# Expert gathers as f32 products straight from the residual, with one more home for weight halves

## The reference

```python
def expert_choice_swiglu(h, w_router, w_gate, w_up, w_down):
    cap = EC_CAPACITY_FACTOR * seq // N_EXPERTS            # 64 tokens per expert, 16 experts
    aff = jax.nn.softmax(jnp.einsum('bsd,de->bse', h, w_router), axis=-1)
    g, idx = lax.top_k(jnp.swapaxes(aff, 1, 2), cap)
    xin = jax.vmap(lambda hb, ib: hb[ib])(h, idx)          # gather
    a = jnp.einsum('becd,edf->becf', xin, w_gate)
    u = jnp.einsum('becd,edf->becf', xin, w_up)
    y = jnp.einsum('becf,efd->becd', jax.nn.silu(a) * u, w_down) * g[..., None]
    return ...zeros.at[idx].add(y)                         # scatter
# x = x + attention part;  x = x + expert_choice_swiglu(rms_norm(x, norm2_g), ...);  rms_norm(x, normf_g)
```

## Time and profile before

| | us |
|---|---|
| time, median of 3 runs | 874.66 (874.02 to 877.3) |
| the profiled execution's own time | 872.47 |
| its span, first to last instruction | 870.7 |
| TensorE busy | 846.2 (97%) |
| VectorE busy | 373.5 (43%) |
| ScalarE busy | 264.8 (30%) |
| GpSimd busy | 29.0 (3%) |
| granted TensorE clock, mean | 0.996 of full speed |
| read from HBM | 235.92 MB |

### The profile page before, as it was taken

How to read it: one execution, slowest core, us unless ns; L and a number is a source line. 1 busy time by engine, 2 the same in 40 slices (tenths; PEclk the granted TensorE clock), 3 DMA queues, 4 the chain that set the end, 5 groups by cost and what they waited for, 6 DMA issues and landing times.

```text
span 870.7 us, 10464 instructions
## 1 busy us (share of the span) xinstructions
PE 846.2 (97%) x4239; PEld 516.6 (59%) x4239; DVE 373.5 (43%) x650; ACT 264.8 (30%) x460; POOL 29.0 (3%) x50
## 2 busy tenths in 40 slices
PE   9999999999999999999999999999999998988996
PEld 8898776687878888888634344344433433334432
DVE  5377977576605335416412146322232231311351
ACT  6234776685634234216011011010100101001231
POOL 1050000000000000001100000000000000000010
PEclk9999999999999999999999999999999999999999
DMA  9730212023133425863999999999999999999996
GB/s 287 172 97 0 74 48 98 1 68 90 43 119 109 118 67 141 293 260 129 424 408 422 428 427 430 427 426 426 429 428 428 429 425 429 427 428 429 425 416 265
DMA packets 81427, 239.20 MB, mean 275 GB/s; under 512 B 8038, under 2 KB 63462, under 8 KB 66788
## 3 DMA queue, kind: packets, MB, share of 16 engines
q1 hardware_dynamic: 75952, 235.94, 68.7%
q10 hardware_dynamic: 5284, 2.09, 1.0%
q0 software_dynamic: 144, 0.51, 0.1%
HBM read 235.92 MB, written 2.62 MB: 274 GB/s over the span
## 4 chain that ended last, share of the span: by engine, by line
PE 79%; DMA 12%; DVE 5%; ACT 2%; issue 1%; POOLq 0%; POOL 0%; SPq 0%; ACTq 0%; DVEq 0%
PE psum L1622 18%; PE psum L1654 11%; PE psum L1150 10%; PE psum L1152 10%; PE psum L1151 10%; DMA wslot<-in_w_down 7%; DMA wslot<-in_w_up 4%; PE psum L1579 3%; PE psum L1673 2%; PE psum L1338 2%; PE psum L1350 2%; PE psum L1782 2%; PE psum L1308 1%; PE psum L1324 1%; DVE w_lo L1855 1%
## 5 line engine op out<-in xcount | busy, mean ns | idle before, releaser
L1622 PE MATMUL psum<-wslot,xinT 128*64 128x512 f32 x1000 | 222.1, 595 | 4.3 <-DMA wslot<-in_w_up 2.5
L1622 PEld LDWEIGHTS psum<-wslot,xinT 128*64 128x64 f32 x1000 | 69.5, 137 | 141.9 <-issue 132.7
L1654 PE MATMUL psum<-wslot,actT 128*64 128x512 f32 x424 | 96.0, 596 | 5.0 <-DMA wslot<-in_w_down 5.0
L1150 PE MATMUL psum<-hT_hi,w_hi 128*128 128x512 f32 x208 | 82.8, 398 | 0.0
L1152 PE MATMUL psum<-hT_hi,w_lo 128*128 128x512 f32 x208 | 81.3, 391 | 0.0
L1151 PE MATMUL psum<-hT_lo,w_hi 128*128 128x512 f32 x208 | 81.3, 391 | 0.0
L1855 DVE TENSOR_TENSOR w_lo<-w_raw,w_hi 128x1024 fp32r<-128x1024 f32 (+1 forms) x46 | 52.9, 1174 | 51.0 <-ACT w_hi L787 50.9
L1654 PEld LDWEIGHTS psum<-wslot,actT 128*64 128x64 f32 x424 | 29.2, 137 | 61.4 <-issue 57.3
L1083 ACT ACTIVATE actT<-psum 128x512 f32<-128x512 f32 x16 | 9.6, 599 | 172.7 <-PE psum L1634 172.7
L2261 DVE TENSOR_TENSOR x<-x,psum 128x512 f32<-128x512 f32 x48 | 29.8, 683 | 57.3 <-PE psum L1673 57.3
L2251 DVE TENSOR_TENSOR y_lo<-psum,y_hi 64x512 fp32r<-64x512 f32 x28 | 19.3, 689 | 81.1 <-ACT y_hi L1093 80.7
(11 more groups left out here) (287 smaller groups left out, 1335.3 us busy)
## 6 DMA issues: line engine op xcount, KB each, us to landing
wslot<-in_w_up SPq DMA_DIRECT2D x27, 2048.0 KB, 23.4
wslot<-in_w_gate SPq DMA_DIRECT2D x25, 2048.0 KB, 24.9
wslot<-in_w_down SPq DMA_DIRECT2D x24, 2048.0 KB, 22.0
w_raw<-in_w_in SPq DMA_DIRECT2D x34, 512.0 KB, 4.7
wslot<-in_w_gate SPq DMA_DIRECT2D x12, 1024.0 KB, 9.2
wslot<-in_w_up SPq DMA_DIRECT2D x9, 1024.0 KB, 10.6
wslot<-in_w_down SPq DMA_DIRECT2D x9, 1024.0 KB, 19.7
w_raw<-in_w_out SPq DMA_DIRECT2D x8, 512.0 KB, 4.9
```

What stands on the lines that cost most here:

```text
L1150: pe.matmul(out_, s_hi, m_hi, start=(k == 0), stop=False)
L1622: mm = pe.matmul(bank[2 * e + n][CAP * f:CAP * f + CAP, :], xinT[:, HALF * h + k, CAP * e:CAP * e + CAP], wslot[place_of(m)][:, k % PART, ...
L1654: mm = pe.matmul(bank[4 + e][CAP * f:CAP * f + CAP, :], actT[:, e, k, CAP * h:CAP * h + CAP], wslot[place_of(m)][:, k % PART, SEQ * f:SEQ ...
```

## The change

It removes the split of the residual. `pick`, `row_ids` and the new `aff_cols` become plain f32, and the gathers multiply pick by x2 itself in f32: 4 products of 512 columns where 8 in fp32r stood. The sums go into a tile of their own, `sums` at W0. The first gather of pair 0 is turned round: chunks of x2 are the stationary operand and pick the moving one, so the result comes transposed, without ACT's copy and TensorE's transposes; it goes chunk by chunk (four, two of them ahead of the gates, two between gate products). The later copies of rows are read by chunks with a step of 4.

The space of `xn_lo` becomes a ninth wide home (W0 + 16), SLOTS = 18, and the two single homes in x2's space move to W0 and W0 + 8. SyncE loads parts 20, 21 and 18 after the first four residual groups, part 19 after the second logits, all ahead of the wait for all groups; half 16 comes one place later.

```diff
-SLOTS = 16
-FIRST_PARTED, LAST_PARTED = (*range(8, 15), 16), range(92, 96)
+SLOTS = 18
+FIRST_PARTED, LAST_PARTED = range(9, 17), range(92, 96)
-EXTRA = {16: 16, 7: 17, 18: 18, 19: 19, 32: 18, 33: 19}
+EXTRA = {16: 18, 7: 19, 18: 20, 19: 21, 32: 20, 33: 21}
-                 enumerate((W0 + 32, 0, 16, W0 + 48, 32, 64, W0 + 64, W0 + 80))]
+                 enumerate((W0 + 32, 0, 16, W0 + 48, 32, 64, W0 + 64, W0 + 80, W0 + 16))]
-    wslot += [sb(f"wslot_once{i}", [PART, D], kib) for i, kib in enumerate((48, 56, 80, 88))]
-
-    xn_hi = sb("xn_hi", [NT, D], W0, F32R)
-    xn_lo = sb("xn_lo", [NT, D], W0 + 16, F32R)
+    wslot += [sb(f"wslot_once{i}", [PART, D], kib) for i, kib in enumerate((48, 56, W0, W0 + 8))]
+
+    sums = sb("sums", [NT, D], W0)
-    pick = sb("pick", [NT, 2, CAP], 100, F32R)
+    pick = sb("pick", [NT, 2, CAP], 100)
...
+        FIRST_BANKS = (6, 7, 4, 5)
...
-            sp.wait_ge(sumsq2, 2)
-            sp.wait_ge(x2_turned, 2)
-            sp.wait_ge(xn_lo_done, 4)
+            sp.wait_ge(proj_done, g_at[("res", 0, NT - 1)] + 1)
+            load_part(20)
+            load_part(21)
             load_part(18)
+            sp.wait_ge(logits_done, 2)
+            load_part(19)
             sp.wait_ge(proj_done, len(groups))
             for m in (7, 11, 12, 13, 14, 15, 16, 17):
                 load_part(m)
-
-            sp.wait_ge(sumsq2, NT + 1)
-            sp.wait_ge(x2_turned, NT + 1)
-            sp.wait_ge(xn_lo_done, 5)
-            sp.wait_ge(xn_lo_pool, len(LOW_BY_POOL))
-            load_part(19)
-            for half in (*range(10, 16), 17, 18, 16, *range(19, len(HALVES) * PAIRS)):
+            for half in (*range(11, 16), 17, 18, 19, 16, *range(20, len(HALVES) * PAIRS)):
...
-                    mm = pe.matmul(into[:, 0:6], pick[:, c, :, :], aff_parts[:, c, p, :, :],
+                    mm = pe.matmul(into[:, 0:3], pick[:, c, :, :], aff_cols[:, c, p, :],
...
+            def gather_first(k, tiles=range(NT)):
+
+                for c in tiles:
+                    pe.wait_ge(pick_done, c + 1)
+                    chunk = x2[:, c, 0:SEQ].rearrange("p (i k) -> p k i", k=HALF)[:, k, :]
+                    mm = pe.matmul(bank[FIRST_BANKS[k]][:, 0:P], chunk, pick[:, c, :, :],
+                                   start=(c == 0), stop=(c == NT - 1))
+                mm.then_inc(xin_turned, 1)
...
                 for c in range(NT):
-                    for part in (xn_hi, xn_lo):
-                        mm = pe.matmul(bank[6 + f][:, :], pick[:, c, :, :], part[:, c, cols],
-                                       start=(c == 0 and part is xn_hi), stop=(c == NT - 1 and part is xn_lo))
+                    mm = pe.matmul(bank[6 + f][:, :], pick[:, c, :, :], x2[:, c, cols],
+                                   start=(c == 0), stop=(c == NT - 1))
...
-                        steps.sort(key=lambda step: step[1] // PART)
+                        steps.sort(key=lambda step: step[1])
...
-            for c in range(NT):
-                pe.wait_ge(pick_done, c + 1)
-                gather_first(c, 0)
-            for c in range(NT - 1):
-                gather_first(c, 1)
-            turn_first_xin(0)
-            gather_first(NT - 1, 1)
+            gather_first(0)
+            gather_first(1)
...
-                    if step == 1:
-                        turn_first_xin(1)
+                    if step in (1, 3):
+                        gather_first(2 + step // 2)
...
-                pe.wait_ge(sum_lo_done, c + 1)
-                for part in (sum_hi, sum_lo):
-                    pe.matmul(row_sum(f), pick[:, c, :, :], part[:, c, SEQ * f:SEQ * f + SEQ],
-                              start=(c == 0 and part is sum_hi), stop=False, skip_group_check=True)
+                pe.matmul(row_sum(f), pick[:, c, :, :], sums[:, c, SEQ * f:SEQ * f + SEQ],
+                          start=(c == 0), stop=False, skip_group_check=True)
...
-                        dve.tensor_reduce(slot_vals[CAP * f:CAP * f + CAP, p % 2, e, :],
-                                          src[CAP * e:CAP * e + CAP, 0:6].rearrange("p (v s) -> p v s", s=2),
-                                          AX, ALU.add).then_inc(slot_aff_done, 1)
+                        dve.tensor_copy(slot_vals[CAP * f:CAP * f + CAP, p % 2, e, :], src[CAP * e:CAP * e + CAP, 0:3])\
+                            .then_inc(slot_aff_done, 1)
...
+                    before = sums if p else x2
+                    dve.tensor_tensor(sums[:, c, cols], before[:, c, cols], bank[added_bank(c, f)][:, :], ALU.add)\
+                        .then_inc(added, 1)
```

## The result

The changed kernel takes 901.29 us (median of 6, 898.6 to 903.09), beside 875.14 us for the kernel before (6 runs): a ratio of 1.0297, with a 95% interval of 1.0278 to 1.0317. It is slower by 26 us. The profiled execution took 898.88 us with a span of 897.0, 26.3 us over the 870.7 of before; the forecast was a span of 895.3, +24.6.

What follows compares the result with a forecast made beforehand. TensorE was taken to bound the kernel until stocked weights ran out in the sixth pair, then transfers. TensorE's +35.5 us less 10.9 us of waits gave +24.6, span 895.3; time 898.5 us, range 889 to 908.

Steps and rivals of the forecast that it cites:

- The race: Expert pairs: TensorE's pair grows from 52.61 to 56.6 us, still under the transfers' 58.8, so the 10.9 us of waits vanish.
- The f32 gather: Double gather of each expert pair on TensorE: 7.24 us in place of 3.76, +3.48 us; seven of them +24.4.
- The small ones: TensorE's smaller additions: pairing of rows +1.0 us, slot values +0.5 each, eight times, +4.0, last gather of rows +3.3.
- Routing: Routing stretch set by TensorE: dropped copies and subtractions gain 0, except the last aff value, -0.3 us.
- the first gather: First pair's gather on TensorE: gates start earlier, -0.5 us; two more chunks between gate products, +1.9 us.
- The sum: Whole span: TensorE's additions +35.5 us less 10.9 us of vanished waits, net +24.6 us, a span of 895.3.
- The step from 899.3 down to 898.5: Final time: lowered from 899.3 us against the median, as a kernel no longer waiting for transfers may vary less.
- The supply: Weight loads: four parts (9.8 us) move into the empty stretch 384 to 404 us; a 3 to 4 us hole after 427.1.
- transfers are some 2.5 us earlier: Net effect on weight transfers: some 2.5 us earlier, with 22 parts rather than 20 in hand when the gates start.
- Rival 1: Transfers set the end and longer gathers hide in TensorE's waits: not slower, 872 us; chance 0.05.
- rival 2: TensorE's waits for weights stay on top, through a late transfer or a larger hole at 427: 910 us; chance 0.08.
- rival 3: Wide f32 products on TensorE cost about 0.33 us a record, 15 us less: 884 us; chance 0.05.

Runs made afterwards that it cites:

- halved loads: Every load after a home's first tenant brings only half its bytes: changed kernel 900.10 us (ratio 1.0301), kernel before 862.67 us (0.9866).

## Why the prediction was right, point by point

**The race.** It rested on two rhythms, 52.6 us a pair on TensorE and 58.8 on the transfers, and on the reading that the 10.9 us of spacing is all that can be hidden. The halved loads gave 10.9 us by the medians and 10.7 by the chain. The pair was forecast at 56.6 us and is 56.4.

**The f32 gather.** Forecast +3.48 us a double gather, measured 6.97 - 3.76 = +3.21. The record is 6.97/16 = 0.436 with its share of the start, near my lower bound of 0.43. The start of 0.1 us was about right; the record of 0.444, half-width products of L1622 taken two at a time, was too long: inside the row six records span 2.74 us and one takes 0.592, which makes 0.429 from start to start. The Trainium skill (FP8 and Floating Point Precision, "TensorE Precision Notes") says that true FP32 takes four passes through the array; the trace comes near it, with 2 x 0.436 us for a product of 512 columns against 0.235 for an fp32r one, 3.7 times.

**The small ones.** Against the earlier trace rows, the slot values and the end:

```profile
828.05 1.09 PE psum L1669 x8
829.14 0.79 PE psum L1672 x8
...
865.55 1.91 PE psum L1678 x4
867.46 0.47 PE psum L1588 x4
867.93 1.72 PE psum L1678 x4
...
880.65 7.02 PE psum L1727 x32
```

Pairing 1.88 (forecast 1.94), slot values 0.79 (0.85), last gather of rows 1.91 + 1.72 + 1.91 + 1.91 = 7.45 in all, +3.1 (+3.3). Not forecast: the strided transposes of the pair, 1.16 in place of 1.02 us.

**Routing.** The aff value that had taken 0.98 us beside POOL takes 0.23 now that POOL's subtraction is gone, and the transpose that needs it follows TensorE's filler products without a wait, as read from the earlier trace rows:

```profile
411.47 0.23 DVE L2041 TENSOR_SCALAR aff_wide<-logit,small 128x16 f32<-128x16 f32 x1
```

The first gather begins at 423.79, not 424.15, though this execution came 0.2 us later into the stage: 0.55 us gained, forecast 0.3.

**The step that was mis-sized: the first gather.** Forecast -0.5 ahead of the gates and +1.9 between them. Measured: 4.00 us where I had 2.2 ahead of the gates, which start 0.9 us later than before and not 0.8 earlier; and 2 x 2.06 - 0.37 = +3.75 between them. Together 3.6 us too little. The fault is in one sentence: that the transposes of L1634 at 0.12 us show a step of 4 to cost nothing. They are transposes, not f32 products, and their loads in the trace of the kernel before already told more, 209 ns with the step (L1634) and 140 without (L1587):

```profile
L1634 PEld LDWEIGHTS psum<-ident,act x64: 196/209/218, 451.3 to 843.5; 128*128 128x128 f32 x64
L1587 PEld LDWEIGHTS psum<-ident,act x32: 138/140/142, 435.8 to 802.1; 128*128 128x128 f32 x32
```

A load that hardly delays the transpose behind it isn't a free load: the step costs a transpose 0.02 us (8 take 1.16 in place of 1.02) and an f32 product of the same 128 columns 0.12.

**The sum.** Over the span: gates 0.9 later; first pair +6.4 (3.75, the single gather 1.6, slot values 0.9 and the rest); six pairs +12.2, which is 22.8 more work less 10.65 of waits; from the seventh gather to the last product +6.9; after it -0.1. Together 26.3 us. The miss of the first gather (3.6) was half offset by the gathers (2) and smaller terms, so the total is closer to its forecast than its terms are. The step from 899.3 down to 898.5, for a kernel that may vary less, has no support: six executions spread over 4.5 us, those of the kernel before over 3.3.

**The supply.** Four parts went into the empty stretch as forecast, and the full transfers end at some 864 us, 24 before the end of TensorE's last product, where I had said 20. The hole after 427 us is larger than my 3 to 4 us: (423 - 160)/428 of 8 us is 4.9 us, and the 45 us after it lose (416 - 376)/428, another 4.2, while SyncE waits for TensorE to free homes. So the step "transfers are some 2.5 us earlier" failed: from 340 to 480 us the changed kernel moves 310 GB/s where the one before moved 316, 2 us of transfer behind. Harmless here, as the halved loads show. Rival 1 (872 us) needed an f32 record near the price of an fp32r one; rival 2 (910) is excluded by the absence of waits; rival 3 (884) by 0.436 us a record.

No run here with whole loads beats the kernel before. Without any limit of supply the changed kernel's TensorE work is at 900, that of its best variant, with the gathers at the old price, at 875, and that of the kernel before at 863: what is left to gain lies in the supply of the kernel before, and no run tried that.

## What to carry over

When two resources run near their limit, find the rhythm of each (the spacing of a group that comes once a round, and bytes over rate) before pricing a change: work added to one is hidden only as far as the other made it wait, here 10.9 of 37 us. Half as many products is not half the time; count records and their shares of time, and look at whether the array is filled. When an operand's step changes, compare its loads with and without the step for the same kind of product: the same step cost a transpose 0.02 us here and an f32 product of equal width 0.12.

## What the runs showed that I had not expected

- The weight load of an f32 product of 128 columns takes 192 ns at step 1, 196 at step 2 and 330 at step 4, and the product 0.128, 0.134 and 0.250 us.
- The start of the span takes some 2.3 to 2.7 us longer in some executions, all of it before 14 us. The first f32 products, which spread a row (four records), in the changed kernel and in the one with 16 places:

```profile
5.41 1.98 PE L1236 MATMUL psum<-g_row,ones 1*128 1x512 f32 x4
```

```profile
5.60 3.78 PE L1234 MATMUL psum<-g_row,ones 1*128 1x512 f32 x4
```

The same four records take twice the time, and the two levels of TensorE's clock are a factor of two apart, 1.2 and 2.4 GHz. The granted clock of that stretch is printed as 1.00 in the longer one, but this is no reading: in the three profiled executions with 3.78 us the trace holds no record of the clock before 13.3 to 13.6 us, in the other seven the first one stands at 4.1 to 6.0 us. From 13.5 us on the products are equally fast in both (1.19 us for eight of the next kind, L1217 and L1215). The lower level thus fits, but it isn't confirmed. Whether this is all of the spread between executions isn't known; those of the changed kernel near 903 us weren't profiled.
